# Second token half of an output norm turned through the up banks, its vector work and the sum of squares placed elsewhere, in a two-block Macaron network on one Trainium2 core

## The reference, cut to what matters

```python
def _rmsnorm(x, g, eps=RMS_EPS):
    xf = x.astype(jnp.float32)
    y = xf * lax.rsqrt(jnp.mean(xf * xf, axis=-1, keepdims=True) + eps)
    return (y * g.astype(jnp.float32)).astype(x.dtype)

def _half_ffn(x, g_pre, g_post, w_gate, w_up, w_down):
    h = _rmsnorm(x, g_pre)
    f = (jax.nn.silu(h @ w_gate) * (h @ w_up)) @ w_down
    return x + 0.5 * _rmsnorm(f, g_post)

for i in range(DEPTH):
    x = _half_ffn(x, ...)
    h = _rmsnorm(x, mix_norm_pre[i])
    m = _conformer_conv(h, ...) if i % 2 == 0 else _diff_attention(h, ...)
    x = x + _rmsnorm(m, mix_norm_post[i])
    x = _half_ffn(x, ...)
```

## Time and profile before

| | |
|---|---|
| median of 3 runs | 2169.89 us (2168.46 to 2170.3) |
| the profiled execution, its own time | 2171.11 us |
| its span, first to last instruction | 2169.3 us |
| mean granted TensorE clock | 0.992 |
| TensorE matmul busy | 2108.2 us, 97% |
| VectorE busy | 1474.7 us, 68% |
| ScalarE busy | 1002.6 us, 46% |
| GpSimd busy | 30.0 us, 1% |
| DMA | 417.46 MB, mean 192 GB/s |

### The profile page before, as it was taken

How to read it: one execution, slowest core, us unless ns; L and a number is a source line. 1 busy time by engine, 2 the same in 40 slices (tenths; PEclk the granted TensorE clock), 3 DMA queues, 4 the chain that set the end, 5 groups by cost and what they waited for, 6 DMA issues and landing times.

```text
span 2169.3 us, 31245 instructions
## 1 busy us (share of the span) xinstructions
PE 2108.2 (97%) x12235; PEld 1839.3 (85%) x12249; DVE 1474.7 (68%) x2059; ACT 1002.6 (46%) x1415; POOL 30.0 (1%) x33
## 2 busy tenths in 40 slices
PE   7999999999999999999999999999999999999998
PEld 5888998888888988888888878878887888988887
DVE  6888878888888647674565457975457546677444
ACT  3434545344443555444353446464345445555443
POOL 0000000000000000000000000010000000001000
PEclk9999999999999999999999999999999999999999
DMA  8788445886787431275545543126554553425552
GB/s 340 297 311 304 166 170 214 318 307 245 290 300 261 155 137 60 80 270 180 187 160 190 192 155 111 65 97 212 177 192 156 193 182 147 156 79 175 194 178 93
DMA packets 75606, 417.46 MB, mean 192 GB/s; under 512 B 5888, under 2 KB 6016, under 8 KB 51840
## 3 DMA queue, kind: packets, MB, share of 16 engines
q1 hardware_dynamic: 75520, 416.27, 53.5%
HBM read 415.20 MB, written 1.05 MB: 192 GB/s over the span
## 4 chain that ended last, share of the span: by engine, by line
PE 89%; DVE 7%; ACT 2%; DMA 1%; issue 1%; SPq 0%; DVEq 0%; ACTq 0%
PE AB L748 13%; PE AB L750 13%; PE AB L749 13%; PE Y L293 9%; PE Y L295 9%; PE Y L294 9%; PE AB L293 2%; PE AB L294 2%; PE AB L295 2%; PE Y L1367 2%; DVE lo L2064 2%; PE N L791 2%; PE M L690 1%; PE Y L748 1%; PE Y L750 1%; PE Y L749 1%
## 5 line engine op out<-in xcount | busy, mean ns | idle before, releaser
L2064 DVE TENSOR_TENSOR lo<-raw,hi 128x2048 fp32r<-128x2048 f32 x310 | 708.1, 2286 | 387.3 <-ACT hi L1517 386.9
L1517 ACT ACTIVATE hi<-raw 128x2048 fp32r<-128x2048 f32 x322 | 615.1, 1914 | 544.6 <-PE Y L295 260.2
L748 PE MATMUL AB<-hi,h_hi 128*128 128x512 f32 x1280 | 506.4, 396 | 1.3 <-DVE lo L2064 1.3
L750 PE MATMUL AB<-hi,h_lo 128*128 128x512 f32 x1280 | 499.2, 390 | 0.0
L749 PE MATMUL AB<-lo,h_hi 128*128 128x512 f32 x1280 | 498.3, 389 | 0.0
L750 PEld LDWEIGHTS AB<-hi,h_lo 128*128 128x128 f32 x1280 | 240.2, 188 | 51.3
L748 PEld LDWEIGHTS AB<-hi,h_hi 128*128 128x128 f32 x1280 | 240.5, 188 | 48.9 <-DVE lo L2064 1.5
L749 PEld LDWEIGHTS AB<-lo,h_hi 128*128 128x128 f32 x1280 | 240.7, 188 | 47.9
L293 PE MATMUL Y<-g_hi,hi 128*128 128x256 f32 x664 | 188.2, 283 | 0.0
L294 PE MATMUL Y<-g_lo,hi 128*128 128x256 f32 x664 | 187.9, 283 | 0.0
L295 PE MATMUL Y<-g_hi,lo 128*128 128x256 f32 x664 | 187.8, 283 | 0.0
(11 more groups left out here) (435 smaller groups left out, 3179.1 us busy)
## 6 DMA issues: line engine op xcount, KB each, us to landing
raw<-slabs SPq DMA_DIRECT2D x322, 1024.0 KB, 5.0
ada_raw<-ada SPq DMA_DIRECT2D x34, 2048.0 KB, 8.2
ada_raw<-ada SPq DMA_DIRECT2D x2, 1024.0 KB, 14.6
kT<-ada SPq DMA_DIRECT2D x1, 1024.0 KB, 10.4
vt<-ada SPq DMA_DIRECT2D x1, 1024.0 KB, 12.4
x<-x_t SPq DMA_DIRECT2D x1, 1024.0 KB, 14.4
out_t<-x SPq DMA_DIRECT2D x4, 256.0 KB, 3.0
vec<-vectors SPq DMA_DIRECT2D x1, 462.0 KB, 3.2
```

Source lines behind the costliest of these rows:

```text
L748: nc.tensor.matmul(out_, h_hi[:, k, at], w_hi, start=start, stop=False)
L750: return nc.tensor.matmul(out_, h_lo[:, k, at], w_hi, start=False, stop=stop)
L1517: nc.scalar.activation(hi[slot][:, :], raw[slot][:, :], ACT.Copy).then_inc(hi_done[slot], 1)
L2064: nc.vector.tensor_tensor(lo[slot][:, :], raw[slot][:, :], hi[slot][:, :].bitcast(F32), ALU.subtract).then_inc(lo_done[slot], 1)
```

## The change

In the feed-forwards with deferred norm (4 to 7), `sums` moves on TensorE from ahead of the first `up` of `step(1)` to behind it, right ahead of `turn_gated`. On VectorE `square_sum` moves from the norm to behind the `lo` of the third slab (not at norm 10, which no feed-forward follows). At norm 9 ScalarE rounds the third slab ahead of the eight squares, and the squares stand behind all eight `h_hi`. In `turn_tokens` the half t=1 goes through the two `AB` banks (`turn_banks`), and its waits for `x_half` are gone, as is the wait for all residuals ahead of the sums of norm 7. On VectorE `second_half` moves ahead of `variance(1)`, which moves ahead of all residuals; at adds 6, 9 and 11 the residuals of t=0 move behind `second(1)`.

```diff
--- before.py
+++ after.py
@@ -478,6 +478,9 @@
         def pair_of(t_, q):
             return t_[:, 2 * q:2 * q + 2, :].rearrange("p k t -> p (k t)")
 
+        def turn_banks(t):
+            return (M, N) if t == 0 else (AB[:, 0, :], AB[:, 1, :])
+
         def token_bank(eng, c, n, q):
 
             if q < 3:
@@ -728,7 +731,6 @@
                 if n in DEFERRED:
                     c.take("sq", KD)
                 elif n >= 6:
-                    pe.wait_ge(x_new, X_BEFORE[6] + KD)
                     stat(KD, ones[1024])
                 elif n:
                     if n == 2:
@@ -854,10 +856,8 @@
             def turn_tokens(n, t):
 
                 i = BY_TOKEN.index(n)
-                for b, bank in enumerate((M, N)):
+                for b, bank in enumerate(turn_banks(t)):
                     pe.wait_ge((yt_act, yt_dve)[b], 2 * i + t + 1)
-                    if t:
-                        pe.wait_ge(x_half, KD * i + KD // 2 * (b + 1))
                     for kk in range(KD // 2):
                         mm = nc.tensor.transpose(bank[:, kk * P:(kk + 1) * P],
                                                  pair_of(kT, 2 * t + b)[:, kk * P:(kk + 1) * P], ident[:, :])
@@ -892,16 +892,15 @@
                     first_up_by_token(8)
                 else:
                     first_up()
-                if f >= 4:
-                    sums([(acc_ready, c.take("acc") + 1, rstd)], ones[1024])
-                    c.take("stat")
-
                 ring = step_slots(c.take("slab", 3 * NSTEP - 3))
 
                 def step(i, ada, first=False, last=False):
                     pe.wait_ge(lo_done[ring[0][0]], i + (ring[0][1] + 1))
                     up(ring[0][0], 0)
                     if first:
+                        if f >= 4:
+                            sums([(acc_ready, c.take("acc") + 1, rstd)], ones[1024])
+                            c.take("stat")
                         turn_gated(i + g0)
                     pe.wait_ge(lo_done[ring[1][0]], i + (ring[1][1] + 1))
                     up(ring[1][0], 1)
@@ -1578,6 +1577,10 @@
                         act.wait_ge(x_new, c["x_new"] - KD + k + 1)
                         nc.scalar.activation(h_hi[:, k, P:T], x[:, k, P:T], ACT.Copy, scale=g[:, k:k + 1]
                                              ).then_inc(hh_ready, 1)
+                    j = c.take("slab")
+                    split(j % 3, j // 3)
+                    c["ahead"] += 1
+                    for k in range(KD):
                         nc.scalar.activation(hf[:, k, :], x[:, k, :], ACT.Square).then_inc(sq_ready, 1)
                     return
                 if n in DEFERRED:
@@ -2266,7 +2269,8 @@
                 if n in DEFERRED:
                     c.take("hh", KD)
                     c.take("h", KD)
-                    square_sum(n)
+                    if n == 10:
+                        square_sum(n)
                     return
                 if n < 6:
                     l, j = divmod(n, 3)
@@ -2330,6 +2334,7 @@
                 next_slab()
                 next_slab()
                 if f >= 4:
+                    square_sum({4: 6, 5: 8, 6: 9, 7: 11}[f])
                     root_of(EPS)
                     c.take("unspread")
                 j0 = c.take("slab", 3 * NSTEP - 4) - 1
@@ -2396,7 +2401,7 @@
                         b, kk = divmod(k, KD // 2)
                         dve.wait_ge(yt_turned, 4 * i + 2 * t + b + 1)
                         at = slice(t * P, (t + 1) * P)
-                        nc.vector.scalar_tensor_tensor(x[:, k, at], (M, N)[b][:, kk * P:(kk + 1) * P], gate[:, k:k + 1],
+                        nc.vector.scalar_tensor_tensor(x[:, k, at], turn_banks(t)[b][:, kk * P:(kk + 1) * P], gate[:, k:k + 1],
                                                        x[:, k, at], ALU.mult, ALU.add).then_inc(x_new if t else x_half, 1)
 
                 def low(t, *ks):
@@ -2412,21 +2417,25 @@
                 variance(0)
                 newton(0)
                 second(0)
-                residual(0, 0, 1)
+                second_half()
                 variance(1)
-                low(0, 0)
-                residual(0, 2, 3)
-                low(0, 1)
-                newton(1)
-                second(1)
                 if n == 8:
-                    second_half()
-                low(0, 2, 3)
-                for k in range(4, KD):
-                    residual(0, k)
-                    if k > 4:
-                        low(0, k - 1)
-                low(0, KD - 1)
+                    residual(0, 0, 1)
+                    low(0, 0)
+                    residual(0, 2, 3)
+                    low(0, 1)
+                    newton(1)
+                    second(1)
+                    low(0, 2, 3)
+                    for k in range(4, KD):
+                        residual(0, k)
+                        if k > 4:
+                            low(0, k - 1)
+                    low(0, KD - 1)
+                else:
+                    newton(1)
+                    second(1)
+                    residual(0, *range(KD))
                 for k in range(KD + 1):
                     if k < KD:
                         residual(1, k)
@@ -2434,8 +2443,6 @@
                         low(1, k - 1)
                         if n == 9:
                             low_half(n + 1, k - 1)
-                    if k == 3:
-                        second_half()
 
             def add(n):
 
```

## The result

| | before | after |
|---|---|---|
| median | 2170.1 us (2168.46 to 2171.52, 4 runs) | 2191.6 us (2190.39 to 2194.77, 4 runs) |
| ratio after to before | | 1.0102, 95% interval 1.0084 to 1.0119 |
| profiled execution, its own time | 2171.11 us | 2190.39 us |
| its span | 2169.3 us | 2188.6 us |
| mean granted TensorE clock | 0.992 | 0.989 |

The change makes the kernel 21.5 us slower, 1.0%; 2192 was forecast, within 2186 to 2197.5.

What follows compares the result with a forecast made beforehand. TensorE, busy 97% of the span, was taken as the bound, so new holes in its queue are paid in full. +15.9 + 3.9 + 5.6 - 3.5 + 0.1 = +22.0 gave 2192 us against the median, range 2186 to 2197.5.

Steps and rivals of the forecast that it cites:

- The uncovered chain: Feed-forwards 4, 5, 7: nothing covers the 5.73 us from sums to gated product; +5.3 us each, +15.9 together.
- The third slab in time: Feed-forwards 4, 5, 7: the third slab's lo ends just before TensorE's first up needs it; 0.1 us kept as bound.
- Feed-forward 6 with add 8: Add 8 through feed-forward 6's transposes: +3.9 us with add 8's gains included, bounds 3.0 and 4.6.
- The clock behind the holes: Four holes of about 5.2 us bring TensorE's clock down: 4 x 1.4 = +5.6 us, lower bound 0.
- my upper bound: Clock term's upper bound: the longer low stretch behind all four holes, 4 x 2.7 us.
- The row of add 8: Clock reading 1.00 over 1638 to 1640: add 8's 1.67 us wait cost nothing, evidence that holes might be free.
- rival 1: The clock doesn't fall behind the four holes: +16.4, 2186.3 us; chance 0.12.
- Add 6 and norm 7: Norm 7's sums start 2.4 us earlier, perhaps at full clock: -3.5 us, bounds -2.4 and -4.7.
- half a chance: Norm 7: if the clock stays up, its 32 records shrink by 2.3 us more; about half was taken.
- Add 9: First residual of t=1 comes 0.14 us later and TensorE waits for it: +0.1 us.
- Add 11: VectorE's 16 residuals set the end and number the same: 0.

Runs made afterwards that it cites:

- The sums in the middle: Changed kernel with the sums in the middle of the first up, 12 of its 24 matmuls in front and 12 behind: 2176.89 us, ratio 1.0027.
- the sums alone: Kernel before with only the sums, the sum of squares and norm 9's rounding of the third slab moved: 2197.73 us, ratio 1.0129.
- the holes filled: Changed kernel with 20 matmuls on zeros into bank N behind the sums in each of the four holes: 2182.65 us, ratio 1.0058.
- the adds alone: Changed kernel with the sums, the sum of squares and norm 9's roundings put back as before: 2162.8 us, ratio 0.9971.
- the gated product first: Changed kernel with VectorE's lo of the next unit behind the gated product in step 1 instead of ahead: 2193.43 us, ratio 1.0109.
- TensorE's sums in their old place: Changed kernel with TensorE's sums back ahead of the first up, VectorE's sum of squares left late: 2177.89 us, ratio 1.0032.

## Why the prediction was right

Point by point, by its own steps:

- *The uncovered chain:* right. +5.3 forecast in feed-forwards 4, 5 and 7, +5.2 measured in each; the hole of 5.2 us was the forecast length. The sums in the middle and the sums alone show that it is this chain and nothing in the adds.
- *The third slab in time:* right. The matmuls of the first `up` in feed-forwards 4, 5 and 7 wait for no `lo`. In feed-forward 5 that `lo` ends at 1456.91 and the `up` starts at 1457.06, so the margin was as thin as worked out.
- *Feed-forward 6 with add 8:* +3.9 forecast, +3.4 measured, within the bounds. The order of the waits was right: `h_lo` 0.55 us (1.67 before), then the slab, 0.82 instead of my 1.4; the third slab's `lo` came 0.5 us sooner than I had worked out.
- *The clock behind the holes:* +5.6 forecast, +7.4 measured off the timelines. The mechanism was right and the size low. I took the shorter low stretch for all four, and only the first had it; the other three had the longer one. I also charged 40% of the whole stretch, by 128-column records. The part in the hole is free and the dense work behind it loses 46%, so three long stretches cost 1.7 to 2.1 us each and not the 2.7 of my upper bound. The filled holes confirm that this time is the clock's. The row of add 8 that spoke against it was read from a stretch that ends 0.2 us behind its hole, but the clock stayed at 1.00 to 1650 as well. A hole of 1.67 us was simply no guide for holes of 5.2, and rival 1 is out. The Trainium skill, "TensorE: Matmul & The Clock Gate", Part 1, has it that the throttled state is the default and activity releases it. The trace after agrees, with 0.57 to 0.66 behind the four holes, and so does the run with the holes filled, with 1.00.
- *Add 6 and norm 7:* -3.5 forecast, -6.3 measured. This is the term that was mis-sized most. The start of the sums was right (-2.4); the clock then stayed up through the sums, which I had given half a chance (-2.5 by 6.36 to 3.84 us), and also through the start of the conformer, 1.4 us which I had not counted at all. Some of this is luck of one execution. Six traces have the same hole of 1.75 us ahead of these sums. In two of them, the kernel after and the sums in the middle, no low clock follows up to the conformer. In the adds alone and the gated product first, 3.4 us of it come behind the sums. In the other two, with the holes filled and with TensorE's sums in their old place, 3.4 us of it fall into the sums, whose 32 records then take 5.47 us. So the 2.4 us of the earlier start are firm, and about 1.5 of the rest come and go. The adds alone gain 6.3 in the median with add 8's share included, with an interval of 3.9 to 8.7.
- *Add 9:* +0.1 forecast, +0.1 measured. *Add 11:* 0 forecast, -0.1 measured.
- *Not foreseen:* +1.6 us between norm 10 and add 10, in unchanged code, where the clock was low for 6.9 us instead of 3.4, and -2.3 ahead of the second block, also unchanged.

The errors of the clock went both ways (+1.8, -2.8, +1.6, -2.3) and nearly cancelled. Between the two profiled executions the change is +19.3 us against a sum of +22.0; between the medians it is +21.5. So 2192 against 2191.6 is closer than the terms deserve, and in part luck. The holes carry the verdict: 15.6 + 3.4 us stand there whatever the clock does.

## What to carry to other kernels

Before moving an instruction to where its operand is ready with ease, follow it forward: what waits for its result, how long that chain is, and which instructions of its own queue lie between. Two cheap matmuls right ahead of a wait for something that hangs on them turned 5.7 us of hidden vector work into a hole of 5.2, four times, while every operand came in time. And moves that come in one bundle are worth running apart: here one half gained 0.3% and the other lost 1.3%.

## What the runs showed of the hardware

The placing of the low-clock stretches isn't a property of the code alone. In the first block, whose code is the same, TensorE's clock was low in different places in the profiled executions of the kernels before and after. Before:

```profile
320.00:328.00 8.00, 7.23 (x38) 0.57 0.25 76
773.00:777.00 4.00, 2.43 (x20) 1.00 0.77 274
```

After:

```profile
320.00:328.00 8.00, 7.49 (x62) 1.00 0.37 131
773.00:777.00 4.00, 4.00 (x24) 0.60 0.91 348
```

So a difference of 2 or 3 us between two single profiles of this kernel can be the clock's alone, and a term that rests on a low stretch needs medians of many runs. The same holds behind holes of one length. The hole of 1.84 us ahead of norm 10 was followed by 3.4 us of low clock in the kernel after and with the sums in the middle. It was followed by none with the adds alone, with the holes filled and with the gated product first. I had also not expected that holes of 2.0 to 3.4 us bring the clock down; in the run with TensorE's sums in their old place all four did.
